# Paged decode attention: the cache page copies that GpSimd issued are issued by the sync queue

## The reference, cut to what matters

```
cache_kv     (N_PHYS, PAGE_SIZE, 4, N_KV_HEADS, HEAD_DIM)  paged rows [cmp_k, cmp_v, slc_k, slc_v]
state_win_kv (DEC_BATCH, WINDOW, 2, N_KV_HEADS, HEAD_DIM)  last window rows [win_k, win_v]
page_table   (DEC_BATCH, PAST_LEN//PAGE_SIZE) int32
...
s_s = einsum('bqkgd,bkqmd->bkgqm', q, k_sel) + b_s
p_s = masked_softmax(s_s, ...)
o_s = einsum('bkgqm,bkqmd->bqkgd', p_s, v_sel)
s_w = einsum('bqkgd,bskd->bkgqs', q, kw) + bias
o_w = einsum('bkgqs,bskd->bqkgd', masked_softmax(s_w, ...), vw)
return g[..., 0:1] * o_c + g[..., 1:2] * o_s + g[..., 2:3] * o_w
```

## Time and profile before

| | before |
|---|---|
| median of 3 runs | 2131.95 us (2129.97 to 2134.59) |
| the profiled execution: its time | 2129.85 us |
| its span in the profile | 2128.1 us |
| PE busy | 1945.2 us (91%) |
| DVE, ACT, POOL busy | 401.2, 260.1, 138.1 us |
| mean granted TensorE clock | 0.93 of full speed |
| moved by DMA | 484.68 MB, 228 GB/s on average |
| page copies of the cache (256 KB each) | 176 issued by SP, 80 by GpSimd |
| SP's queue, ACT's queue, GpSimd's queue | 392.40, 45.66, 45.15 MB |

### The profile page before, as it was taken

One profiled execution on the slowest core, in us unless ns is written; L12 is line 12 of the kernel. 1 busy time (PEld: TensorE's weight loads), 2 busy tenths in 40 slices (PEclk: granted clock), 3 DMA queues, 4 the chain that ended last, 5 costly groups with the idle time before them and its releaser, 6 DMA issues.

```text
span 2128.1 us, 36327 instructions
## 1 busy us (share of the span) xinstructions
PE 1945.2 (91%) x15417; PEld 1562.4 (73%) x15417; DVE 401.2 (19%) x930; ACT 260.1 (12%) x565; POOL 138.1 (6%) x198
## 2 busy tenths in 40 slices
PE   6799998999999978786786999999999999999995
PEld 5589986777767765554566969788796959697882
DVE  3795022000010025543422000000000000000002
ACT  1000011000000114433312000000000000000001
POOL 2071001200000010023201000000000000000001
PEclk9899998999999965678897999999999999999997
DMA  9755655944734224067763979999898979798994
GB/s 243 199 161 161 206 182 175 382 139 138 277 127 111 73 89 167 1 210 254 235 160 115 295 264 343 303 297 311 284 319 277 328 266 340 263 343 304 293 312 162
DMA packets 353746, 484.68 MB, mean 228 GB/s; under 512 B 32548, under 2 KB 310062, under 8 KB 353004
## 3 DMA queue, kind: packets, MB, share of 16 engines
q1 hardware_dynamic: 325600, 392.40, 58.0%
q10 hardware_dynamic: 14924, 45.66, 6.5%
q0 software_dynamic: 13120, 45.15, 6.1%
HBM read 450.51 MB, written 40.98 MB: 231 GB/s over the span
## 4 chain that ended last, share of the span: by engine, by line
issue 46%; PE 42%; DMA 4%; DVE 3%; ACT 2%; another core or an unknown queue 1%; ACTq 1%; POOL 0%; SPq 0%; DVEq 0%; POOLq 0%
PE ps L1415 14%; PE ps L1445 7%; PE ps L1539 4%; PE ps L1561 3%; DMA arena<-in_state_win_kv 3%; PE ps L1580 2%; PE ps L1598 1%; PE ps L1644 1%; PE ps L1722 1%; PE ps L1630 1%; PE ps L1786 1%; PE ps L1383 1%; ACT arena L864 1%; PE ps L1661 1%
## 5 line engine op out<-in xcount | busy, mean ns | idle before, releaser
L1871 PEld LDWEIGHTS ps<-arena 128*128 128x128 f32 x5632 | 633.1, 192 | 5.2 <-issue 5.1
L1871 PE MATMUL ps<-arena 128*128 128x128 f32 x5632 | 633.4, 275 | 1.3 <-ACT arena L899 1.3
L1415 PE MATMUL ps<-arena 128*128 128x288 f32 x1216 | 303.8, 414 | 20.8 <-DMA arena<-in_conv_w_pw 15.7
L1881 PE MATMUL ps<-arena 128*128 128x512 f32 x704 | 304.2, 593 | 1.7 <-DVE arena L1327 1.7
L1415 PEld LDWEIGHTS ps<-arena 128*128 128x128 f32 x1216 | 235.2, 194 | 88.7 <-DMA arena<-in_conv_w_pw 14.9
L1881 PEld LDWEIGHTS ps<-arena 128*128 128x128 f32 x704 | 133.1, 190 | 168.1 <-issue 168.1
L1327 DVE TENSOR_TENSOR arena<-arena,ps 128x256 f32<-128x256 f32 x88 | 37.1, 421 | 883.1 <-ACT arena L915 883.1
L1445 PE MATMUL ps<-arena 64*64 64x128 f32 x4096 | 160.4, 313 | 5.0 <-issue 5.0
L1445 PEld LDWEIGHTS ps<-arena 64*64 64x64 f32 x4096 | 156.1, 248 | 9.0 <-issue 8.4
L1007 DVE SCALAR_TENSOR_TENSOR arena<-arena 128x256 f32<-128x256 f32 x240 | 119.9, 578 | 0.0
L915 ACT ACTIVATE arena<-ps 128x256 f32<-128x256 f32 x88 | 33.8, 384 | 531.1 <-PE ps L1871 531.0
(11 more groups left out here) (298 smaller groups left out, 1161.5 us busy)
## 6 DMA issues: line engine op xcount, KB each, us to landing
arena<-in_moe_w_gate SPq DMA_DIRECT2D x88, 1024.0 KB, 6.5
arena<-in_moe_w_up SPq DMA_DIRECT2D x88, 1024.0 KB, 7.2
arena<-in_moe_w_down SPq DMA_DIRECT2D x88, 1024.0 KB, 4.9
arena<-in_cache_kv SPq DMA_DIRECT2D x176, 256.0 KB, 5.5
arena<-in_cache_kv POOLq DMA_DIRECT2D x80, 256.0 KB, 7.1
xg_scratch<-arena POOLq DMA_DIRECT2D x26, 512.0 KB, 17.6
arena<-in_conv_w_pw SPq DMA_DIRECT2D x12, 1024.0 KB, 14.1
arena<-in_cmp_w ACTq DMA_DIRECT2D x6, 2048.0 KB, 21.8
```

The costliest lines, as they stand in the source:

```text
L1415: ins = mm(dst, w[:, k, c * P:(c + 1) * P], rhs[:, k, :], start=(k == 0), stop=(k == KD - 1))
L1871: ins = mm(dst, w[:, k, c * P:(c + 1) * P], XeT[:, k, :], start=(k == 0), stop=(k == KD - 1))
L1881: ins = mm(ps[:, 4 + c, :], He[:, 2 * k + kk, :], w[:, kk, 512 * c:512 * (c + 1)], start=(k == 0 and kk == 0), stop=(k == 10 and kk == 1))
```

## The change

Units with odd numbers go from GpSimd's loop to SP's, in the order of their numbers; GpSimd's loop is gone. `kv_unit`, the waits in it, the buffers and what all other engines do are unchanged.

```diff
@@ -501,7 +501,7 @@
             sp.wait_ge(sem("xg_zero"), 26 * 16)
             sp.wait_ge(sem("y_put"), 16 * 16)
             for pr in range(PAIRS):
-                for u in range(0, 10, 2):
+                for u in range(10):
                     kv_unit(sp, page, pr, u)
             sp.wait_ge(sem("kt_tr"), 10 * PAIRS)
             weights(START["wout"], START["wout"] + 2)
@@ -587,10 +587,6 @@
 
             gp.wait_ge(sem("xg_zero"), 26 * 16)
             gp.wait_ge(sem("y_put"), 16 * 16)
-            for pr in range(PAIRS):
-                for u in range(1, 10, 2):
-                    kv_unit(gp, page, pr, u)
-
             gp.wait_ge(sem("wout_done"), 1)
             gain = a["norm_final"]
             gp.dma_start(gam, bass.AP(tensor=gain.tensor, offset=gain.offset, ap=[[0, P], [1, D]])).then_inc(sem("gam_in"), 16)
```

## The result

| | before | after |
|---|---|---|
| median | 2131.8 us (14 runs) | 2140.75 us (14 runs) |
| ratio to before | 1 | **1.0037**, 95% interval 1.0021 to 1.0053 |
| the profiled execution: time, span | 2129.85, 2128.1 us | 2139.09, 2137.3 us |

The kernel is slower by 0.37%, some 8 us. 2140.75 us lies in the predicted range of 2125 to 2142, close to its end, and the sign is the forecast's, but the forecast (+1.9 us) had about a quarter of the size. "The same" had been given the largest chance (0.47), and the time is above the 2136.2 us from which the prediction counts it as slower (0.36).

The account below looks back on a forecast made before the run. PE, busy 91%, waits in decode attention for units 5 to 9; SP's issue would become the stream's limit. Four pairs to their last scores take 109.2 us instead of 107.3; 1.9 on the 2131.95 median gives 2134 us, range 2125 to 2142.

Parts of the forecast that it names:

- The same: Whole kernel: time between 2127.7 and 2136.2 us, counted as no change; chance 0.47.
- rival A: Decode attention: SP bounds the whole pair at 5.1 us a unit; 9.4 us slower, 2141 us; chance 25%.
- The pitch: SP's loop: a page unit takes 4.5 us, page-number loads included, against 3.0 us for its bytes.
- S: Decode attention: moment PE has transposed a request pair's first unit, freeing the staging slot unit 5 waits for.
- Waits: PE after S: wait for unit 5 below 1 us, waits of 1 to 3.5 us each for units 6 to 9.
- Unit 9 at S+21.4: Decode attention: second window unit landed 21.4 us after S, with ends at S+20.8 and S+22.3.
- The tail after unit 9: PE from unit 9's landing to the pair's last score: 5.9 us, between 5.1 and 6.7 us.
- the stage: Decode attention: time from S to the last score, four pairs together; 107.3 us before, forecast 109.2 us.
- Second half of a pair, and Pool: SP's units 10 to 14 hidden behind softmax and products, 4 us to spare; relieving Pool worth nothing.
- The rate: Decode attention transfers: less than 300 GB/s between S and S+15.
- Rival B: Decode attention: transfer rate stays the limit, only the order improves; 14.9 us faster, 2117 us; chance 10%.
- Rival C: Decode attention: Pool's copies slow SP's, so unit 9 comes at S+20; 6.9 us faster, 2125 us; chance 10%.

## Why the prediction was right, and where it was off

The mechanism was right and the size was not. The measured 2140.75 us lies inside the range by 1 us, and the late end of the forecast's own sum, 2131.95 + 8.7 = 2140.65 us, stops just short of it. That the time fell inside is in part luck: the end of the range was set by rival A.

**The pitch.** Right: 4.5 us a unit, without a copy of units 5 to 7 held up; these units of pair 1 were issued at S+0.3, S+4.8 and S+9.3, where S+0.2, S+4.7 and S+9.2 stood. Doubling and hoisting the loads moved the time both ways as computed.

**Waits.** Right in kind: the wait for unit 5 shrank and others came for units 6, 7 and 9, though none for unit 8. Their size was not: in pairs 2 and 3 unit 5 still cost 1.23 and 1.92 us where less than 1 was named, and unit 7 cost 4.26 to 5.61 us where at most 3.5 was.

**Unit 9 at S+21.4: the term that was mis-sized.** It was 22.3 to 23.4, mean S+22.8, beyond even the late end of S+22.3. The 5.6 us from first issue to the whole unit hold for unit 5 in pair 1 (5.5 us), while unit 6 took 6.2 there and unit 5 in pair 3 took 7.0. Unit 7's slowest copy in pair 1 took 5.9 us, not 4.0, with the window copies right behind it, so unit 7 was there at S+16.9 in pair 1 instead of S+14.8. I had taken the four copies from the start of a burst (4.0 us) and dismissed the trailing of later ones, 5.4 us in the median of the same burst. That it is the windows' copies that hold it was not tried by itself, and the traces fit in the main. In the second trace of the changed kernel the slowest copy of unit 7 takes 5.8, 5.6 and 5.3 us in pairs 1 to 3, and no copy of units 5 and 6, with nothing close behind them, more than 4.7. Against it stand unit 7 of pair 0 (4.4 us in the first trace, with the windows behind it too) and unit 5 of pair 3 there (5.3 us, with nothing behind it). So the cause stays open in part. 1.4 us in each of four pairs are 5.6 of the missing us.

**The tail after unit 9.** I took 5.9 us for a lower clock. It was 6.8 us in pair 0 and 5.2 us in the other three, where unit 9's transposes take 1.09 us, as at the higher clock; the term was 1.2 us too long over the four pairs, so the sum was 4.4 us short in all, 113.6 for 109.2. That is the stage's share of the nearly 7 us between 2134 and 2140.75. The rest lies outside the stage in the traces, or in the 107.3 us from which the sum counted: they came from one trace, and the second gave 104.8.

**Second half of a pair, and Pool.** Right: PE waited for none of units 0 to 4 of pairs 1 to 3, and the time from the last score to the next S stayed at 16 to 16.6 us.

**The rate.** Below 300 GB/s between S and S+15, as named: 212 to 215 in the four pairs. It is a weak sign, since the kernel before has 267 GB/s there in pair 1.

**Rival A.** Its figure of 2141 us was hit by luck, not by its mechanism: the pitch was 4.5 us, not 5.1, and SP did not bound the pair. That only happens with the loads doubled.

**Rival B.** The changed kernel does not behave so. With the loads out of the way its idea holds in part: 99.5 us, against 92.4 computed, because SP's burst does not run at 348 GB/s from the first copy on: in pair 1 it moves 230 GB/s over the first 8 us behind S and 351 over the next 10.

**Rival C.** Its premise is right, more than I gave it: with GpSimd's copies beside them, SP's land up to 5.5 us later (3.8 against 9.3 us in the run with the windows on GpSimd). A queue of SP alone accounts for a part of that: twelve copies in 6.6 us, in the run with the numbers ahead, land within 6.7 us. It brought nothing here, since SP's issue was the limit once GpSimd's copies were gone.

## What to carry to other kernels

Before moving transfers to one queue, add up what the issuing engine does per transfer, register loads and waits included, and set it against the time of the bytes; here 4.5 us stood against 3.0. What can be computed before a wait belongs before it, and what doesn't need the awaited buffer can be fetched before it too. With two queues at work, put what is needed last into the queue that yields, not the one that overtakes: here the windows on SP (0.9979), where page units on SP and windows on GpSimd gave 1.0078.

## What the runs showed of the hardware that was not expected

- Two queues don't share by the order of asking. In one trace SP's copies of 256 KB land in 2.7 to 3.8 us with nothing beside them and in 5.8 to 9.3 us beside GpSimd's windows, and in the run with half units SP's window copies took 14.2 and 15.2 us, GpSimd's, asked for after them, 8.6 and 9.8 us.
- The same copies are cut into packets of 1 KB in SP's queue and of 3.3 KB in GpSimd's, on average.
- GpSimd as the only issuer is some 4 us slower than SP as the only one: 1.0074 against 1.0037, with a pitch of 4.6 against 4.5 us from unit 5 to unit 6, though a copy holds it for 714 ns against 373.
